# Two products that advance together, chunk by chunk, in a two-block transformer kernel on one Trainium2 core

## The chip, the core and the metric

The kernel runs on one core of one Trainium2 chip. The metric is device time in microseconds (us) of one execution. Engines are named as in the profile: PE is TensorE, DVE is VectorE, ACT is ScalarE, POOL is GpSimd, SP is SyncE.

## What is computed

The input is a sequence of 256 tokens of width 1024 and a context of 256 tokens, all in fp32. The first block has two hybrid layers; the second block has two rounds of feed-forward, mixer, feed-forward.

```
hybrid layer: shift, scale, gate = split(silu(c) @ ada_w + ada_b)
  hx = rms_norm(x) * (1 + scale) + shift          (the same for the context y)
  rq, rk, rv, rg, nq, nk, nv, ng, gq, gk, gv, gg, mg = split(hx @ w_in)
  x += gate * ((g_ret*(ret @ w_ret_o) + g_na*(na @ w_na_o) + g_gqa*(gqa @ w_gqa_o)) @ w_out)
  (the context is updated in layer 0 only)
x = rms_norm(x, final_norm_w)
for i in (0, 1):
  h += 0.5 * swiglu(rms_norm(h), ffn1_w_in[i], ffn1_w_out[i])
  h += mixer_i(rms_norm(h))     i=0: (gelu(y) * rg_lru(conv(r))) @ rec_w_out;  i=1: (u * sg) @ sg_w_out
  h += 0.5 * swiglu(rms_norm(h), ffn2_w_in[i], ffn2_w_out[i])
return rms_norm(h, final_norm)
```

## The kernel before

**Products.** Everything that feeds a product lies transposed: 128 features on the partitions, tokens along the row, eight chunks (KC = 8) of 128 features. A weight tile is 128 x 1024 fp32, that is, one output block of 128 features with its eight chunks. To keep fp32 accuracy, weights and activations are each split into a rounded high part and a low rest, and each chunk is three matmuls into one PSUM bank (`three`, L2211-2217): w_hi by h_hi (L2215), w_hi by h_lo (L2216), w_lo by h_hi (L2217). The moving side has 512 columns (256 tokens and 256 of context) in layer 0 and for keys and values in layer 1, else 256.

**Weight tiles.** SP loads each tile into one of six raw buffers. ACT makes w_hi (L1446) into one of four slots; from the fifth tile on it waits until PE has used the tile four before (semaphore `tile_used`). DVE makes w_lo (L1723), and PE waits for it (`lo_ready`). The schedule puts splits three tiles ahead of the product (`split_ahead`, L329).

**Banks.** Products alternate between the two PSUM banks G[0] and G[1]; a product waits on its first chunk until its bank was evacuated (`g_free`). Sums and spreads of the norms use bank M, the ffn's second up-product the banks S, the adaptive-scale products the banks T.

**Order.** `build_schedule` (L714) records one list of steps, and every engine walks the same list and emits its own part of each step, so the order of the list is the order on each engine. `product` (L368) adds one product: it calls `split_ahead`, then `flush` puts the steps that were held back (evacuations of the product before, squares), then the product in parts of 3, 3 and 2 chunks, between which due and background steps come.

**The start.** Eight `pair` steps bring the adaptive scale and shift of one chunk each: 32 small matmuls of the ada weights (L2289, that is 64 in the trace with their passes), a transpose of the result on DVE (L1751) and an add (L1759, `ada_a`). The first norm's sums are spread over the partitions in M, copied to `rstd` (L1793, in `norm_spread_step`), and `prescale` makes m = x * rstd per chunk (L1741). `normed` then makes h_hi and h_lo of a chunk: h_hi by ACT (L1476 where the chunk's `how` is "dve", L1483 after a full-precision m on ACT), h_lo by DVE (L1867, L1862 before it if `how` is "dve"). Between pairs `keep_busy` lets PE multiply a constant (L2258, n matmuls of 512 columns in fp32r). While `hold` is set, a product comes in parts of 2, 3, 3 chunks, and pair 7 with the `normed` of chunks 6 and 7 (`last_pair`, L758) stands behind the first part of the first product. Until then only tile 0 is split.

**Layers.** `schedule_layer` (L394) makes, for each of four groups of the neighbourhood branch, the products nk, nv (512 columns), nq, ng. The evacuation of nk ("key", to k_s) is ACT L1491 then DVE L1930; that of nv ("value") is ACT L1503 to `stage`. At the end of a layer the eight w_out products are followed by the residual, a square (L1456) and adds of squares; `rms` (L652) then has PE sum the squares over partitions (`norm_mean`, L2327), DVE and POOL take the root (L1801, L1316), and PE spreads it (`norm_spread`, L2345). In layer 1 the eight `normed` steps follow, all chunks with `how` "act". Beside these, POOL loads and adds a bias table (L1277, 128 x 768).

**Feed-forward.** `ffn_step` (PE, L2475) runs 22 rounds of two ups (gate into G, the other into S) and a down. The first two ups are up(0, g) and then up(0, u) (L2528-2529), then the norm's sums and, within up(1, g), its spread. ACT's part splits tile t0+3 after the first up and t0+4 after the second (L1619-1620); DVE's part is at L2090.

**Mixers.** `mixer_out` (L911) makes eight output products from mix_hi and mix_lo (L1663, L2153), whose chunks come out of the scans (recurrent) or the gating (spatial), each followed by a residual add (L1922). In the recurrent mixer, y_act (L1817) evacuates the last y product.

## Time and profile before

| | |
|---|---|
| median of 3 runs | 2062.36 us (2061.68 to 2063.36) |
| the profiled execution | 2060.16 us, span 2058.4 us |
| mean granted PE clock | 0.983 of full speed |
| busy: PE / DVE / ACT / POOL | 1980.5 / 1121.9 / 892.9 / 246.1 us |
| chain that ended last, PE's share | 56%, on 18 + 17 + 17% the three lines of `three` |
| DMA | 289.28 MB, 141 GB/s on average, 317 GB/s in the first fortieth |

The span is that of the trace; the execution's own time is 1.8 us more. Busy time counts compute instructions only; an engine's idle time is what it waited, and the trace names for each idle stretch the instruction whose semaphore ended it. The granted clock is the share of TensorE's full 2.4 GHz that the throttle gave; 0.50 is 1.2 GHz.

### The profile page before, as it was taken

Reading aid. Unit: us, or ns where it says so; the run is one execution under the profiler, and the core shown is the slowest. Engines: PE = TensorE matmul, PEld = TensorE weight load, DVE = VectorE, ACT = ScalarE, POOL = GpSimd, SP = SyncE. Lnnn points to the kernel's source line nnn. Section 1 sums busy time; section 2 is a strip of 40 time slices with the busy share of each in tenths; the row PEclk is TensorE's granted clock in tenths of the full one; section 3 lists DMA queues with packets and bytes.
Section 4 is the critical chain, followed back from the end, with each engine's and each line's share of the span. In section 5 each row is a group of like instructions: output and inputs, shape, how many; then the busy total and the mean of one; then the engine's idle time right before and its main releaser. Section 6 shows DMA issues by size and latency. Waiting matters only on the chain.

```text
span 2058.4 us, 37778 instructions
## 1 busy us (share of the span) xinstructions
PE 1980.5 (96%) x14537; PEld 1782.1 (87%) x14537; DVE 1121.9 (55%) x1798; ACT 892.9 (43%) x1431; POOL 246.1 (12%) x269
## 2 busy tenths in 40 slices
PE   8999999999999899998999999989999999999998
PEld 6777887777787688888899999979999999999998
DVE  6554443445433655446556556875556555675554
ACT  5444231344422544334445445654445444554443
POOL 1000010111012100201121001311001000200000
PEclk9999999999999899999999999989999999999999
DMA  8221433311234323333354555435555555445553
GB/s 317 72 67 63 146 140 133 123 52 62 76 98 144 106 99 103 103 134 103 117 180 145 184 184 173 134 124 180 182 183 190 184 183 184 145 152 175 184 183 113
DMA packets 79432, 289.28 MB, mean 141 GB/s; under 512 B 8912, under 2 KB 9168, under 8 KB 79312
## 3 DMA queue, kind: packets, MB, share of 16 engines
q1 hardware_dynamic: 77616, 281.61, 41.1%
q0 software_dynamic: 1120, 4.72, 0.7%
q8 instruction: 89, 1.46, 0.3%
q10 hardware_dynamic: 576, 1.24, 0.2%
q14 instruction: 31, 0.25, 0.0%
HBM read 286.49 MB, written 1.05 MB: 140 GB/s over the span
## 4 chain that ended last, share of the span: by engine, by line
PE 56%; DVE 5%; ACT 3%; issue 2%; POOL 1%; POOLq 0%; DVEq 0%; ACTq 0%
PE bank L2215 18%; PE bank L2217 17%; PE bank L2216 17%; DVE w_lo L1723 1%; ACT w_hi L1446 1%; PE bank L2404 1%; PE bank L2387 1%; PE bank L2373 1%; ACT h_hi L1462 0%; PE bank L2345 0%; ACT m L1476 0%; PE bank L2444 0%; POOL stats L1316 0%; DVE r_conv L2148 0%; ACT mix_hi L1663 0%
## 5 line engine op out<-in xcount | busy, mean ns | idle before, releaser
L2215 PE MATMUL bank<-h_hi,w_hi 128*128 128x256 f32 (+1 forms) x2720 | 870.5, 320 | 22.4 <-DVE h_lo L1808 7.6
L2217 PE MATMUL bank<-h_hi,w_lo 128*128 128x256 f32 (+1 forms) x2720 | 846.9, 311 | 0.0
L2216 PE MATMUL bank<-h_lo,w_hi 128*128 128x256 f32 (+1 forms) x2720 | 846.4, 311 | 0.0
L1723 DVE TENSOR_TENSOR w_lo<-raw,w_hi 128x1024 fp32r<-128x1024 f32 x484 | 600.4, 1244 | 415.5 <-ACT w_hi L1446 415.0
L1446 ACT ACTIVATE w_hi<-raw 128x1024 fp32r<-128x1024 f32 x484 | 508.9, 1055 | 503.3 <-PE bank L2217 450.0
L2215 PEld LDWEIGHTS bank<-h_hi,w_hi 128*128 128x128 f32 x2720 | 518.8, 191 | 80.4 <-issue 41.7
L2217 PEld LDWEIGHTS bank<-h_hi,w_lo 128*128 128x128 f32 x2720 | 519.3, 191 | 28.9
L2216 PEld LDWEIGHTS bank<-h_lo,w_hi 128*128 128x128 f32 x2720 | 520.2, 191 | 23.3 <-issue 0.4
L2215 PE MATMUL bank<-hid_hi,w_hi 128*128 128x256 f32 x704 | 198.0, 281 | 2.1 <-DVE hid_lo L2071 2.1
L2217 PE MATMUL bank<-hid_hi,w_lo 128*128 128x256 f32 x704 | 197.5, 280 | 0.0
L2216 PE MATMUL bank<-hid_lo,w_hi 128*128 128x256 f32 x704 | 197.2, 280 | 0.0
L1351 POOL TENSOR_TENSOR silu_g<-silu_g,rstd 128x256 f32<-128x256 f32 x88 | 65.3, 742 | 639.9 <-ACT silu_g L1598 639.9
L2215 PEld LDWEIGHTS bank<-hid_hi,w_hi 128*128 128x128 f32 x704 | 132.8, 189 | 3.0 <-DVE w_lo L1723 2.2
L2216 PEld LDWEIGHTS bank<-hid_lo,w_hi 128*128 128x128 f32 x704 | 132.8, 189 | 0.0
L2217 PEld LDWEIGHTS bank<-hid_hi,w_lo 128*128 128x128 f32 x704 | 132.4, 188 | 0.0
L2065 DVE TENSOR_TENSOR hidden<-silu_g,bank 128x256 f32<-128x256 f32 x88 | 37.0, 421 | 122.4 <-POOL silu_g L1351 119.9
L1598 ACT ACTIVATE silu_g<-silu_g 128x256 f32<-128x256 f32 x88 | 36.8, 418 | 154.0 <-DVE silu_g L2056 154.0
L1536 ACT ACTIVATE work<-bank,row_stat 128x512 f32<-128x512 f32 (+1 forms) x96 | 58.3, 612 | 68.9 <-DVE row_stat L1951 68.9
L1546 ACT ACTIVATE work<-bank 128x512 f32<-128x512 f32 (+1 forms) x96 | 45.4, 524 | 79.5 <-PE bank L2387 79.2
L1951 DVE TENSOR_REDUCE row_stat<-bank 128x1 f32<-128x512 f32 (+1 forms) x96 | 53.1, 594 | 34.6 <-PE bank L2373 34.5
L1316 POOL TENSOR_TENSOR stats<-stats,neg_half 128x2 f32<-128x2 f32 (+2 forms) x21 | 24.1, 1146 | 340.4 <-DVE stats L1801 340.4
L1311 POOL TENSOR_TENSOR m<-m,square 128x512 f32<-128x512 f32 (+1 forms) x32 | 33.3, 1042 | 220.3 <-DVE square L1897 220.3
(232 smaller groups left out, 2143.5 us busy)
## 6 DMA issues: line engine op xcount, KB each, us to landing
raw<-in_weights SPq DMA_DIRECT2D x516, 512.0 KB, 3.3
early<-in_first SPq DMA_DIRECT2D x10, 512.0 KB, 13.7
bias<-in_rpb POOLq DMA_DIRECT2D x8, 384.0 KB, 3.4
early_o<-in_first SPq DMA_DIRECT2D x4, 512.0 KB, 16.8
x<-in_tokens SPq DMA_DIRECT2D x2, 512.0 KB, 5.4
x<-in_tokens ACTq DMA_DIRECT2D x2, 512.0 KB, 8.0
work<-in_first SPq DMA_DIRECT2D x2, 512.0 KB, 16.6
out<-cols_out SPq DMA_DIRECT2D x4, 256.0 KB, 2.1
```

The costliest lines, as they stand in the source:

```text
L1311: pool.tensor_tensor(v, v, branch_sum[:, st.dc % 2, 0:st.cols], ALU.add).then_inc(added, 1)
L1351: pool.tensor_tensor(v, v, rstd[:, 0:SEQ], ALU.mult).then_inc(silu_scaled, 1)
L1446: nc.scalar.activation(w_hi[:, n % SPLIT, :], raw[:, t % RAW, :], ACT.Copy).then_inc(hi_ready, 1)
L1536: nc.scalar.activation(probs[:, hp, 0:u.keys], S[use % 2][:, 0:u.keys], ACT.Exp, bias=row_stat[:, 0, i:i + 1], accum_out=row_stat[:, 1, i: ...
L1546: nc.scalar.activation(probs_t[:, hp, 0:u.keys], T[use % 2][:, 0:u.keys], ACT.Copy)\
L1598: nc.scalar.activation(silu_g[:, i % 2, :], silu_g[:, i % 2, :], ACT.Silu).then_inc(silu_ready, 1)
L1723: dve.tensor_tensor(w_lo[:, t % RAW, :], raw[:, t % RAW, :], w_hi[:, SPLIT_NO[t] % SPLIT, :].bitcast(F32), ALU.subtract).then_inc(lo_ready, 1)
L1951: dve.tensor_reduce(row_stat[:, 0, i:i + 1], s[:, 0:u.keys], AX_X, ALU.max, negate=True)\
L2065: dve.tensor_tensor(hidden[:, i % 2, :], silu_g[:, i % 2, :], S[i % 2][:, 0:SEQ], ALU.mult)\
L2215: nc.tensor.matmul(dst, w_hi[:, SPLIT_NO[t] % SPLIT, at], hi, start=start, stop=False, skip_group_check=shared)
L2216: nc.tensor.matmul(dst, w_hi[:, SPLIT_NO[t] % SPLIT, at], lo, start=False, stop=False, skip_group_check=shared)
L2217: return nc.tensor.matmul(dst, w_lo[:, t % RAW, at], hi, start=False, stop=stop, skip_group_check=shared)
```

## The change

1. `product_pair` records two products whose chunks alternate, chunk 0 of the first, chunk 0 of the second, chunk 1 of the first, and so on, in both G banks. It is used for nk and nv of the first group in both layers and for the first two of the eight output products of both mixers. In the four ffns `first_ups` does the same with up(0, g) in G[0] and up(0, u) in S[0].
2. `norm_part` (PE): in both layers, behind the last w_out product, PE multiplies the sum of the earlier squares first and then, in `norm_mean`, only the last square.
3. The adaptive norm's copy of the spread root (L1793) is gone; `prescale` multiplies x by the bank M itself, and the last prescale frees M.
4. In layer 1 chunks 0 and 4 are made by DVE ("dve") rather than by ACT.
5. `keep_busy` takes fp32 operands and counts of 11, 2, 1, 1, 1, 1 where it had 38, 7, 3, 3, 3, 3 in fp32r, and three more such matmuls stand in layer 1 behind the spread.
6. Pair 7 and the `normed` of chunks 6 and 7 stand before the first product; the parts 2, 3, 3 are gone.

```diff
+    def product_pair(self, whats, src, n, norm=None, **fields):
+        jobs = []
+        for i, what in enumerate(whats):
...
+        self.split_ahead(self.tile)
+        self.flush()
+        for k in range(KC):
+            for job in jobs:
+                self.add("product", job=job, at=k, part=1, base=0)
+            if k in (2, 5, 7):
+                self.part_done()
+                self.fill()
+        self.tile += 2
+        return jobs
...
-        key("nk", g)
-        value("nv", g)
+        jobs = s.product_pair(("nk", "nv"), n=BOTH, **src()) if c == 0 else [None, None]
+        key("nk", g, jobs[0])
+        value("nv", g, jobs[1])
...
+        if dc == KC - 1:
+            norm.cols = live
+            norm_part(s, norm)
...
-        st.how = "act" if norm.layer or k % 2 == 0 else "dve"
+        st.how = "dve" if k in ((0, 4) if norm.layer else (1, 3, 5, 7)) else "act"
...
-    def last_pair():
-        normed(s, norm, 6)
-        pair(7)
-        normed(s, norm, 7)
-        s.hold = False
-        s.split_ahead(0)
-
-    s.background = [last_pair]
+    normed(s, norm, 6)
+    pair(7)
+    normed(s, norm, 7)
+    s.hold = False
     for layer in range(DEPTH):
         if layer:
             norm.how, norm.layer = "ada", layer
             s.add("ada_scale", layer=layer)
             rms(s, norm)
+            s.keep_busy(3, s.tile)
...
 def mixer_out(s, what, mixer, weight):
...
+    jobs = s.product_pair((what, what), n=SEQ, src="mix", mixer=mixer)
     for n in range(KC):
-        job = s.product(what, n=SEQ, src="mix", norm=None, mixer=mixer)
+        job = jobs[n] if n < 2 else s.product(what, n=SEQ, src="mix", norm=None, mixer=mixer)
...
-                    dve.wait_ge(m_free, norm.m_spread + 1)
-                dve.tensor_tensor(m[:, k, :], x[:, k, :], rstd[:, :], ALU.mult).then_inc(prescaled, 1)
+                    dve.wait_ge(m_full, norm.m_spread + 1)
+                dve.tensor_tensor(m[:, k, :], x[:, k, :], M[:, :], ALU.mult).then_inc(prescaled if k < KC - 1 else m_free, 1)
...
+                def first_ups():
...
+                    for k in range(KC):
+                        pe.wait_ge(h_lo_ready, norm.chunks[k].h + 1)
+                        for which, bank in (("g", G), ("u", S)):
+                            ins = three(bank[0][:, 0:SEQ], (t0 + ffn_tile(which, 0), k), h_hi[:, k, 0:SEQ], h_lo[:, k, 0:SEQ],
+                                        k == 0, k == KC - 1)
...
-                up(0, "g", first=True)
-                up(0, "u")
+                first_ups()
```

How this moves instructions is shown at three places. **PE at the start, before**: the small L2289 matmuls are the ada pairs (pair 6, then pair 7, whose weights are in `work`), L2215 to L2217 are the chunks of nk; nv begins 26 rows further down.

```order
L2289 MATMUL bank<-early_o,c_silu 32x64 [waits t_free0,first_landed6]
L2289 MATMUL bank<-early_o,c_silu 32x64 x31
L2215 MATMUL bank<-h_hi,w_hi 128x512 [waits h_lo_ready,lo_ready]
L2216 MATMUL bank<-h_lo,w_hi 128x512
L2217 MATMUL bank<-h_hi,w_lo 128x512
L2215 MATMUL bank<-h_hi,w_hi 128x512 [waits h_lo_ready]
L2216 MATMUL bank<-h_lo,w_hi 128x512
L2217 MATMUL bank<-h_hi,w_lo 128x512
L2289 MATMUL bank<-work,c_silu 32x64 [waits t_free1,first_landed7]
L2289 MATMUL bank<-work,c_silu 32x64 x31
L2215 MATMUL bank<-h_hi,w_hi 128x512 [waits h_lo_ready]
L2216 MATMUL bank<-h_lo,w_hi 128x512
```

**PE at the start, after** (the lines of `three` are now L2251 to L2253, those of the pairs L2329):

```order
L2329 MATMUL bank<-early_o,c_silu 32x64 [waits t_free0,first_landed6]
L2329 MATMUL bank<-early_o,c_silu 32x64 x31
L2329 MATMUL bank<-work,c_silu 32x64 [waits t_free1,first_landed7]
L2329 MATMUL bank<-work,c_silu 32x64 x31
L2251 MATMUL bank<-h_hi,w_hi 128x512 [waits h_lo_ready,lo_ready]
L2252 MATMUL bank<-h_lo,w_hi 128x512
L2253 MATMUL bank<-h_hi,w_lo 128x512
L2251 MATMUL bank<-h_hi,w_hi 128x512 [waits lo_ready]
L2252 MATMUL bank<-h_lo,w_hi 128x512
L2253 MATMUL bank<-h_hi,w_lo 128x512
L2251 MATMUL bank<-h_hi,w_hi 128x512 [waits h_lo_ready]
L2252 MATMUL bank<-h_lo,w_hi 128x512
```

Pair 7 stands before the first chunk, and behind the first chunk of nk stands the first chunk of nv with a wait for its own weight tile, ahead of all other chunks.

**ACT at the end of the start, before**: h_hi of chunk 7, the high parts of weight tiles 1 to 5 (raw buffers 1 to 5), and the evacuations of nk (`k_s`) and nv (`stage`).

```order
L1476 ACTIVATE h_hi<-m,ada,ada_a 128x256 [waits a_ready,prescaled]
L1476 ACTIVATE h_hi<-m,ada,ada_a 128x256
L1446 ACTIVATE w_hi<-raw 128x1024 [waits raw_landed1]
L1446 ACTIVATE w_hi<-raw 128x1024 [waits raw_landed2]
L1446 ACTIVATE w_hi<-raw 128x1024 [waits raw_landed3]
L1446 ACTIVATE w_hi<-raw 128x1024 [waits tile_used,raw_landed4]
L1491 ACTIVATE k_s<-bank 128x512 [waits tile_used]
L1446 ACTIVATE w_hi<-raw 128x1024 [waits tile_used,raw_landed5]
L1503 ACTIVATE stage<-bank 128x512 [waits tile_used]
```

After:

```order
L1508 ACTIVATE h_hi<-m,ada,ada_a 128x256 [waits a_ready,m_free]
L1508 ACTIVATE h_hi<-m,ada,ada_a 128x256
L1478 ACTIVATE w_hi<-raw 128x1024 [waits raw_landed1]
L1478 ACTIVATE w_hi<-raw 128x1024 [waits raw_landed2]
L1478 ACTIVATE w_hi<-raw 128x1024 [waits raw_landed3]
L1478 ACTIVATE w_hi<-raw 128x1024 [waits tile_used,raw_landed4]
L1478 ACTIVATE w_hi<-raw 128x1024 [waits tile_used,raw_landed5]
L1523 ACTIVATE k_s<-bank 128x512 [waits tile_used]
L1535 ACTIVATE stage<-bank 128x512 [waits tile_used]
```

The high part of tile 5 (raw buffer 5), which waits until nv's tile has been used, stands now before the evacuation of nk.

**DVE at the same place, before**: the arithmetic of pair 7, h_lo of chunk 7, the low parts, and the last step of nk's evacuation.

```order
L1751 STREAM_TRANSPOSE merge_tanh<-bank 128x64 [waits ada_set,t_full]
L1756 TENSOR_TENSOR ada<-merge_tanh,par 128x2x2 [waits t_free1]
L1759 SCALAR_TENSOR_TENSOR ada_a<-ada,par 128x2 [waits ada_set]
L1862 TENSOR_SCALAR scaled<-m,ada_a,ada 128x256 [waits a_ready,prescaled]
L1862 TENSOR_SCALAR scaled<-m,ada_a,ada 128x256
L1867 TENSOR_TENSOR h_lo<-scaled,h_hi 128x512 [waits h_hi_ready,shift_dve]
L1723 TENSOR_TENSOR w_lo<-raw,w_hi 128x1024 [waits hi_ready] x4
L1930 SCALAR_TENSOR_TENSOR k_s<-bank,k_s 128x512 [waits qk_hi]
L1723 TENSOR_TENSOR w_lo<-raw,w_hi 128x1024 [waits hi_ready]
```

After:

```order
L1783 STREAM_TRANSPOSE merge_tanh<-bank 128x64 [waits ada_set,t_full]
L1788 TENSOR_TENSOR ada<-merge_tanh,par 128x2x2 [waits t_free1]
L1791 SCALAR_TENSOR_TENSOR ada_a<-ada,par 128x2 [waits ada_set]
L1898 TENSOR_SCALAR scaled<-m,ada_a,ada 128x256 [waits a_ready,m_free]
L1898 TENSOR_SCALAR scaled<-m,ada_a,ada 128x256
L1903 TENSOR_TENSOR h_lo<-scaled,h_hi 128x512 [waits h_hi_ready,shift_dve]
L1755 TENSOR_TENSOR w_lo<-raw,w_hi 128x1024 [waits hi_ready] x5
L1966 SCALAR_TENSOR_TENSOR k_s<-bank,k_s 128x512 [waits qk_hi]
L1909 COPY v_s<-bank 128x512 [waits m_full]
L1755 TENSOR_TENSOR w_lo<-raw,w_hi 128x1024 [waits hi_ready]
```

Five low parts (tiles 1 to 5) stand between h_lo of chunk 7 and the evacuation of nk, where four stood. The order of h_lo of chunk 7 and the first of them is the same.

## Rows read from the trace of the kernel before

**Rows 1.** Page, parts 1 (busy) and 5 (groups: busy, mean ns).
```profile
PE 1980.5 (96%) x14537; PEld 1782.1 (87%) x14537; DVE 1121.9 (55%) x1798; ACT 892.9 (43%) x1431; POOL 246.1 (12%) x269
...
L1723 DVE TENSOR_TENSOR w_lo<-raw,w_hi 128x1024 fp32r<-128x1024 f32 x484 | 600.4, 1244 | 415.5 <-ACT w_hi L1446 415.0
```

**Rows 2.** PE's waits, whole span: us in total, times, longest us.
```profile
PE bank L2215 <- DVE h_lo L1867: 6.7, 3, 5.0
```

**Rows 3.** Timeline, PE, the start: start, length, instruction, [idle before <- releaser].
```profile
33.32 0.73 PE L2215 MATMUL bank<-h_hi,w_hi 128*128 128x512 f32 x1
33.85 0.63 PE L2216 MATMUL bank<-h_lo,w_hi 128*128 128x512 f32 x1
34.27 0.63 PE L2217 MATMUL bank<-h_hi,w_lo 128*128 128x512 f32 x1
...
36.11 1.42 PE L2289 MATMUL bank<-work,c_silu 128*32 128x64 f32 x64
...
42.04 0.39 PE L2215 MATMUL bank<-h_hi,w_hi 128*128 128x512 f32 x1
...
47.48 0.47 PE L2215 MATMUL bank<-h_hi,w_hi 128*128 128x512 f32 x1
```

**Rows 4.** Timeline of DVE at the start, same columns.
```profile
37.61 0.25 DVE L1751 STREAM_TRANSPOSE merge_tanh<-bank 128x64 f32<-128x64 f32 x1 [0.93 <-PE bank L2289]
...
40.42 6.31 DVE L1723 TENSOR_TENSOR w_lo<-raw,w_hi 128x1024 fp32r<-128x1024 f32 x4 [0.19 <-ACT w_hi L1446]
46.66 0.68 DVE L1930 SCALAR_TENSOR_TENSOR k_s<-bank,k_s 128x512 fp32r<-128x512 f32 x1
```

**Rows 5.** Timeline of ACT at the start.
```profile
38.35 1.09 ACT L1476 ACTIVATE h_hi<-m,ada,ada_a 128x256 fp32r<-128x256 f32 x2 [2.41 <-DVE ada_a L1759]
39.35 2.94 ACT L1446 ACTIVATE w_hi<-raw 128x1024 fp32r<-128x1024 f32 x3
```

**Rows 6.** Windows of 1 us: busy (count) by engine, PE clock, DMA share, GB/s.
```profile
425.00:426.00 1.00, 0.71 (x6) 0.71 (x7) 0.63 (x2) 0.02 (x1) 0.00 (x0) 0.98 0.00 0
428.00:429.00 1.00, 1.00 (x4) 0.71 (x4) 0.55 (x3) 0.91 (x4) 0.00 (x0) 0.50 0.00 0
429.00:430.00 1.00, 1.00 (x6) 0.55 (x4) 0.68 (x3) 0.11 (x2) 0.00 (x0) 0.81 0.00 0
```

**Rows 7.** Timeline of PE where layer 1 begins.
```profile
679.97 0.76 PE L2215 MATMUL bank<-h_hi,w_hi 128*128 128x512 f32 x1 [5.04 <-DVE h_lo L1867]
...
696.74 0.28 PE L2215 MATMUL bank<-h_hi,w_hi 128*128 128x256 f32 x1
```

**Rows 8.** Timeline of DVE where layer 1 begins.
```profile
674.97 0.69 DVE L1793 COPY rstd<-bank 128x512 f32<-128x512 f32 x1 [3.33 <-PE bank L2345]
675.69 3.52 DVE L1741 TENSOR_TENSOR m<-x,rstd 128x512 f32<-128x512 f32 x3
...
683.14 1.94 DVE L1867 TENSOR_TENSOR h_lo<-m,h_hi 128x512 fp32r<-128x512 f32 x1 [0.32 <-ACT h_hi L1483]
...
689.74 0.69 DVE L1867 TENSOR_TENSOR h_lo<-m,h_hi 128x512 fp32r<-128x512 f32 x1 [0.96 <-ACT h_hi L1483]
```

**Rows 9.** Timeline of PE, spread of the second norm in the first ffn.
```profile
1096.97 0.60 PE L2345 MATMUL bank<-con,stats 128*128 128x128 f32 x4
```

**Rows 10.** Timeline of PE at the recurrent mixer's output products.
```profile
1347.94 0.55 PE L2215 MATMUL bank<-mix_hi,w_hi 128*128 128x256 f32 x1 [3.64 <-DVE y_act L1817]
...
1359.55 0.58 PE L2215 MATMUL bank<-mix_hi,w_hi 128*128 128x256 f32 x1 [0.37 <-DVE mix_lo L2153]
```

**Rows 11.** Timeline of DVE, same place.
```profile
1352.81 0.42 DVE L1817 TENSOR_TENSOR y_act<-bank,rstd 128x256 f32<-128x256 f32 x1
...
1360.02 1.23 DVE L1723 TENSOR_TENSOR w_lo<-raw,w_hi 128x1024 fp32r<-128x1024 f32 x1 [0.52 <-ACT w_hi L1446]
```

**Rows 12.** Timeline of ACT in the second ffn's beginning.
```profile
1385.33 1.06 ACT L1446 ACTIVATE w_hi<-raw 128x1024 fp32r<-128x1024 f32 x1 [0.49 <-PE bank L2217]
```

**Rows 13.** Timeline of PE at the spatial mixer's output products.
```profile
1834.95 0.38 PE L2215 MATMUL bank<-mix_hi,w_hi 128*128 128x256 f32 x1 [1.07 <-DVE mix_lo L2153]
```

More of the change, by code:

```diff
@@ L313, in add, with keep_busy @@
         return step
-    def keep_busy(self, n):
-        self.add("busy", part=n)
+    def keep_busy(self, n, tile=None):
+        self.add("busy", part=n, tile=tile, job=self.uses.get("G", 0))
     def add_after_split(self, kind, **fields):
@@ L655, in rms, with norm_part @@
     norm_spread(s, norm)
+def norm_part(s, norm):
+    norm.m, norm.part = s.use("M"), True
+    s.add("norm_part", norm=norm)
 def norm_mean(s, norm):
+    if norm.m is not None:
+        norm.rows = s.count("rows")
+        s.add("norm_mean", norm=norm)
+        return
     norm.m, norm.rows = s.use("M"), s.count("rows")
@@ L726, in scale @@
             prescale(s, norm, k)
-    s.keep_busy(38)
+    s.keep_busy(11)
     pair(0)
-    s.keep_busy(7)
+    s.keep_busy(2)
     norm_mean(s, norm)
@@ L736, in build_schedule @@
     pair(2)
-    s.keep_busy(3)
+    s.keep_busy(1)
     normed(s, norm, 0)
@@ L742, in build_schedule @@
     pair(3)
-    s.keep_busy(3)
+    s.keep_busy(1)
     normed(s, norm, 2)
@@ L746, in build_schedule @@
     pair(4)
-    s.keep_busy(3)
+    s.keep_busy(1)
     normed(s, norm, 3)
@@ L750, in build_schedule @@
     pair(5)
-    s.keep_busy(3)
+    s.keep_busy(1)
     normed(s, norm, 4)
@@ L2252, in busy_step @@
             def busy_step(st):
-                if st.n == 0:
+                if st.tile is None:
                     pe.wait_ge(set_up_busy, 1)
-                ones = w_hi[:, SPLIT - 1, 0:BOTH]
+                    some = w_hi[:, SPLIT - 1, 0:BOTH].bitcast(F32)
+                else:
+                    pe.wait_ge(lo_ready, SPLIT_NO[st.tile] + 1)
+                    pe.wait_ge(g_free[st.job % 2], st.job // 2)
+                    some = w_hi[:, SPLIT_NO[st.tile] % SPLIT, 0:BOTH].bitcast(F32)
                 for _ in range(st.part):
-                    nc.tensor.matmul(G[0][:, :], ones[:, 0:P], ones, start=True, stop=True)
+                    nc.tensor.matmul(G[st.job % 2][:, :], some[:, 0:P], some, start=True, stop=True)
             def ada_tile_step(st):
@@ L2306, in norm_spread_step, with norm_part_step @@
                 norm_spread(st.norm)
+            def norm_part_step(st):
+                norm = st.norm
+                c = norm.cols
+                pe.wait_ge(m_free, norm.m)
+                pe.wait_ge(sq_added, norm.units[-2].add_n + 1)
+                for b in range(c // P):
+                    nc.tensor.matmul(M[:, b:b + 1], square_of(norm.units[0])[:, P * b:P * b + P], C_("ones"),
+                                     start=b == 0, stop=False, skip_group_check=True)
             def norm_mean(norm):
                 c, halves = norm.cols, norm.units[0].blocks
+                if norm.part:
+                    last_unit = norm.units[-1]
+                    pe.wait_ge(squared, last_unit.n + 1)
+                    for b in range(c // P):
+                        ins = nc.tensor.matmul(M[:, b:b + 1], square_of(last_unit)[:, P * b:P * b + P], C_("ones"),
+                                               start=False, stop=b == c // P - 1, skip_group_check=True)
+                    ins.then_inc(m_full, 1)
+                    return
                 if norm.m:
@@ L2491, in up @@
                     for k in range(KC):
-                        if first:
-                            pe.wait_ge(h_lo_ready, norm.chunks[k].h + 1)
                         if spread and k == 5:
```

40 lines of the change are left out of this document (26 added, 14 removed).

## The prediction

> **What bounds the kernel now.** I read the page's busy times first: PE is busy 1980.5 of 2058.4 us [rows 1], so at most 78 us can be won, and only at places where PE waits. The table of PE's waits comes next; its largest entry among the products is one wait of 5.0 us for h_lo L1867 [rows 2]. Then the timelines around each place that the change touches: the start, the beginning of layer 1, the ffns' first ups, the mixers' outputs. Everywhere else PE runs product after product, so a microsecond lost or won on PE is one of the kernel's. The question at each place is which wait ends last: the activations, the weight tile or the bank.
>
> Two prices recur. A matmul of 512 columns starts every 0.42 us at the lower clock (33.85 to 34.27) and every 0.227 us at the higher (24 of them from 42.04 to 47.48) [rows 3]; a chunk of three is 1.26 or 0.68 us, so each microsecond at half clock costs 0.46. And after an idle of about 2 us near 424 the granted clock was 0.50 (1.2 GHz) in 428 to 429 and 0.81 in 429 to 430 on the way back to full [rows 6], with PE busy all that time. I charge **3.5 us at half clock, 1.6 us of work**, per new long wait, with ends of 0 and of 3.1 (6.8 us at half).
>
> **The start.** Before, nk's first chunk starts at 33.32, pair 7 at 36.11 behind two chunks, and nv runs from 42.04 to 47.48, where nq follows at once [rows 3]. The changed order puts pair 7 ahead of nk, and the second chunk product on PE is nv's chunk 0, which needs w_lo of tile 1. That stands on ACT behind h_hi of chunk 7 and on DVE behind h_lo of chunk 7, as before, so PE stands still until the whole chain of pair 7 is through. The chain: the transpose started at 37.61, 1.50 after pair 7 [rows 4]; h_hi(7) at 38.35, w_hi from 39.35 [rows 5]; w_lo from 40.42 [rows 4]; a w_lo takes 1.24 [rows 1], so tile 1 was whole at 41.7, 5.6 after pair 7's start. Pair 7 now starts at 33.4; but DVE idled only 0.93 before that transpose [rows 4], so the chain moves up by 0.93, to 40.7, unless DVE's queue ahead of it moves too (then at best 33.4 + 5.6 = 39.0). PE does one chunk by 36 and waits some 4.7 us. Then 15 chunk products are left: 10.2 us at the full clock, 51.0; with 1.6 for half clock, 52.6.
>
> Now the banks. Before, nk's bank was evacuated while nv ran. Advanced together, both end at once, and nq needs G[0]. By the order of ACT and DVE, w_hi and w_lo of tile 5 come ahead of k_s. Tile 4's w_hi can start when nk is done, 0.68 before nv, plus about 0.3 until the matmul has drained; two w_hi are 2 x 0.98 (three take 2.94) [rows 5], then w_lo 1.24 [rows 1] and k_s 0.68 [rows 4], with about 0.1 for the handing over: -0.4 + 1.96 + 1.24 + 0.68 + 0.1, or **3.6 us of idle PE** after nv. nq starts at 56.2 against 47.48: +8.8 (52.6 + 3.6 = 56.2, rounded up for the first matmul). After that second wait another 1.6 at half clock: **+10.4**. Ends: 7.1 with no half clock at all, 13.4 with 6.8 us of it twice. ACT's evacuation of nk lies beside w_lo of tile 5 and costs nothing. Smaller keep_busy counts cost and give nothing: those matmuls stood between waits for the ada weights' DMA.
>
> **Beginning of layer 1.** Before, PE starts nk at 679.97 after 5.04 of waiting and nq at 696.74 [rows 7]. norm_part brings nothing: w_lo and the ada tile's arithmetic on DVE held the root anyway. The rstd copy goes, 0.69 [rows 8]. h_lo of chunk 7 stood at 689.74 [rows 8] behind ACT's h_hi (it idled 0.96 for it); with chunks 0 and 4 made on DVE, ACT is relieved and DVE loaded with two more passes, and I leave its end at 690.4. Behind it two chunk products remain, 1.4, and some 0.4 of backlog, 692.2. The bank wait follows as at the start, 3.6: nq at 695.8, 0.9 earlier. Half clock after it, 1.6: **+0.7, taken as +1**. Ends: -2.8 (no loss of clock, and chunk 7 by the 1.5 of the next paragraph earlier), and +5 where the clock stays down until 688 as it did, since 16 chunks at 1.26 don't fit there.
>
> A term inside this: three prescales took 3.52 where an operation of that size took 0.69, so 1.5 too long, and one h_lo took 1.94 instead of 0.69 [rows 8]; both times POOL was adding its bias table. The changed prescale reads M in PSUM and one operand from SBUF. I take no gain from it, since h_lo keeps its two SBUF operands. The Trainium skill, "GPSIMD Engine Reference", section 1, says that GpSimd's SBUF interfaces are shared with VectorE, with contention for DVE instructions that have two SBUF inputs. By that rule the changed prescale would no longer be held up, and layer 1 would come out 1.5 us lower, and the sum at +5.5.
>
> **First ffn.** up(0, g) trickled, with three small waits, and DVE and the root follow; the spread was at 1096.97 [rows 9]. norm_part takes the sums off the path (0.44: half of its matmuls), the pair fills the trickle. The root's step stands behind two w_lo on DVE, 2.5 us [rows 1], so it can't come by more than the DVE chain does. **-1.1**, ends 0 and -2.5.
>
> **Recurrent mixer's output.** The first product waits 3.64 until 1347.94, then for mix_lo up to 1359.55 [rows 10]; it ends with a chunk of 256 columns, 0.64 at half clock (three times half of 0.42), at 1360.2, and the second, eight such chunks less what comes at full clock, near 1365.0. Now the second can't start before G[1] is free, which y_act does at 1352.81 + 0.42 [rows 11]. From 1353.3 fifteen chunks of 256 columns at 0.64 would end at 1362.9, and a part at full clock makes it 1361.7. The third product's bank waits for a residual that stands behind a w_lo at 1360.02 + 1.23 [rows 11], about 1361.7 too. **-3.3**, ends -2.1 and -4.4.
>
> **Other ffns and the spatial mixer.** In the second and fourth ffn up(0, g) had no waits. The pair only makes its tile's slot come free with up(0, u): ACT's w_hi at 1385.33 [rows 12] starts some 2.3 later, then w_lo, the root, the spread: **+0.4 each** (0 to +0.8). The third has two small waits but its DVE chain sets the spread: 0. The spatial mixer loses its wait of 1.07 [rows 13] and keeps 0.25 for a residual: **-0.8** (0 to -1.1).
>
> **Sum.** 10.4 + 1 - 1.1 - 3.3 + 0.8 - 0.8 = +7.0 on the profiled 2060.16, 2067.2. The median of the runs is 2.2 above that execution: **2069.4**. What a measurement here can tell from no change is about 0.2%, 4.1 us, so the edges are 2058.2 and 2066.5.
>
> **Rivals.**
> - *Faster.* Chunk 7's chain decides, at the start. If what stands on DVE ahead of the transpose moves up as well (the copy and the fp32 fillers are gone), tile 1 is whole at 39.0 and PE's wait is 3 us; if then the clock holds, the start costs 7.1 - 1.7 = 5.4, and the pairs elsewhere, at full clock, give their best ends: 5.4 - 2.8 - 2.5 - 4.4 - 1.1 = -5.4, **2057.0**. It takes over once the clock keeps full through waits of 3 us; the row of 428 to 429 [rows 6] speaks against. Chance 0.09.
> - *No difference.* The order is as said, but the clock doesn't fall at the two bank waits: 7.0 - 3.2 = +3.8, **2066.2**; with a start chain at 39.0, less. Chance 0.20.
> - *As forecast.* Chance 0.58.
> - *Worse.* The clock stays at half for 6.8 us after each wait, and layer 1's pair is bound by PE at half clock: 13.4 + 3 - 1.1 - 2.1 + 0.8 - 0.5 = +13.5, **2075.9**. Chance 0.13.
>
> **Range.** 2062 to 2077 leaves out most of the first rival and little above. The forecast's own range is 2066.5 to 2073. Faster 0.09, same 0.20, slower 0.71.
>
> **What would show it.** PE waits of 4 to 5 us for w_lo between nk's and nv's chunk 0 near 36 to 41, and of about 3.6 us for k_s between nv and nq, both at the start and near 692. nq of layer 0 at 56, of layer 1 some 9 us later than before. No gap for mix_lo after 1353 of the old time. The prediction is wrong in its main term if tile 1 is split before pair 7's chain ends, if k_s comes before the high part of tile 5, or if the granted clock is full right after these waits.

## The result and the profile after

| | before | changed |
|---|---|---|
| median of 5 runs | 2062.36 us (2060.56 to 2063.39) | 2074.2 us (2072.25 to 2074.91) |
| ratio | | 1.0056, 95% interval 1.0041 to 1.0071 |
| span of the profiled execution | 2058.4 us | 2073.2 us |
| mean granted PE clock | 0.983 | 0.982 |

The change makes the kernel **11.8 us slower** by the medians. The two profiled executions lie 14.8 us apart, so a ledger of the traces has to come to 14.8.

The page of the changed kernel, its busy times and the group of PE with the new waits (columns as in [rows 1]):

```profile
PE 1989.1 (96%) x14520; PEld 1783.7 (86%) x14520; DVE 1122.0 (54%) x1800; ACT 891.6 (43%) x1429; POOL 244.7 (12%) x269
...
L2251 PE MATMUL bank<-h_hi,w_hi 128*128 128x256 f32 (+1 forms) x2720 | 872.1, 321 | 26.9 <-DVE k_s L1966 7.5
```

PE is busy 8.6 us longer than before (1989.1 against 1980.5) with the same products. Most of it is the fillers, 23.7 us against 16.8, with three new ones in layer 1:

```profile
L2258 PE MATMUL bank<-w_hi 128*128 128x512 f32 x57 | 16.8, 447 | 1.4 <-POOL w_hi L1257 1.4
L2298 PE MATMUL bank<-w_hi 128*128 128x512 f32 x40 | 23.7, 738 | 1.4 <-POOL w_hi L1289 1.4
```

The first line is the kernel before, the second the changed one. The time at half clock, summed over the whole trace, is 69 us before and 76 us after, so the clock makes most of the rest of the 8.6. The remaining 6.2 of the 14.8 is more idle time. PE's waits (us in total, times, longest):

```profile
PE bank L2251 <- DVE k_s L1966: 7.5, 2, 3.9
...
PE bank L2251 <- DVE w_lo L1755: 5.9, 2, 4.0
...
PE bank L2251 <- DVE h_lo L1903: 1.4, 3, 0.6
```

The wait for h_lo in the adaptive norm fell from 6.7 [rows 2] to 1.4, but nothing came sooner by it: the new fillers stand in that time, and nk's first chunk in layer 1 starts 7.14 us after the spread (687.42 to 694.56), before 7.12 (672.85 to 679.97). New are 7.5 for k_s and 4.0 of the 5.9 for w_lo, 11.5 together; a wait of 1.9 for w_lo was there before.

The start, timeline of PE:

```profile
34.02 0.67 PE L2329 MATMUL bank<-early_o,c_silu 128*32 128x64 f32 x28 [2.09 <-issue]
...
34.51 2.00 PE L2329 MATMUL bank<-work,c_silu 128*32 128x64 f32 x63
...
42.07 0.79 PE L2251 MATMUL bank<-h_hi,w_hi 128*128 128x512 f32 x1 [4.04 <-DVE w_lo L1755]
...
59.31 0.77 PE L2251 MATMUL bank<-h_hi,w_hi 128*128 128x512 f32 x1 [3.93 <-DVE k_s L1966]
```

DVE, first pair 6's transpose in the kernel before, then the changed kernel from the same transpose on:

```profile
33.44 0.25 DVE L1751 STREAM_TRANSPOSE merge_tanh<-bank 128x64 f32<-128x64 f32 x1 [1.03 <-PE bank L2289]
```

```profile
34.84 0.25 DVE L1783 STREAM_TRANSPOSE merge_tanh<-bank 128x64 f32<-128x64 f32 x1 [1.71 <-PE bank L2329]
...
37.99 0.24 DVE L1783 STREAM_TRANSPOSE merge_tanh<-bank 128x64 f32<-128x64 f32 x1
...
39.91 0.69 DVE L1903 TENSOR_TENSOR h_lo<-scaled,h_hi 128x512 fp32r<-128x512 f32 x1 [0.45 <-ACT h_hi L1508]
40.79 5.17 DVE L1755 TENSOR_TENSOR w_lo<-raw,w_hi 128x1024 fp32r<-128x1024 f32 x3 [0.18 <-ACT w_hi L1478]
56.20 2.36 DVE L1755 TENSOR_TENSOR w_lo<-raw,w_hi 128x1024 fp32r<-128x1024 f32 x2 [10.24 <-ACT w_hi L1478]
58.48 0.68 DVE L1966 SCALAR_TENSOR_TENSOR k_s<-bank,k_s 128x512 fp32r<-128x512 f32 x1
```

ACT:

```profile
38.72 1.09 ACT L1508 ACTIVATE h_hi<-m,ada,ada_a 128x256 fp32r<-128x256 f32 x2 [1.38 <-DVE ada_a L1791]
39.72 2.94 ACT L1478 ACTIVATE w_hi<-raw 128x1024 fp32r<-128x1024 f32 x3
55.11 2.00 ACT L1478 ACTIVATE w_hi<-raw 128x1024 fp32r<-128x1024 f32 x2 [12.46 <-PE bank L2253]
```

Read them together. Pair 7 starts at 34.51; its transpose at 37.99, without idle before it, behind DVE's own queue, which pair 6 had made 1.4 late (34.84 against 33.44); h_hi of chunk 7 at 38.72; then the high parts at 39.72, the low parts at 40.79; PE's first chunk of nv comes at 42.07 after 4.04 us of waiting for w_lo. At the end of the pair the two high parts (2.00 from 55.11), two low parts (from 56.20) and k_s (58.48) stand one behind the other, and nq starts at 59.31 after 3.93. Before, nq started at 47.48 [rows 3]: 11.8 later. The granted clock (windows, columns as in [rows 6]):

```profile
38.00:41.00 3.00, 0.03 (x1) 0.00 (x0) 2.19 (x8) 2.28 (x4) 0.00 (x0) 1.00 0.37 141
42.00:48.00 6.00, 5.93 (x14) 4.68 (x15) 3.96 (x3) 0.65 (x1) 2.22 (x2) 0.50 0.23 68
60.00:65.00 5.00, 5.00 (x14) 3.84 (x13) 0.00 (x0) 0.00 (x0) 0.00 (x0) 0.50 0.00 0
```

After each of the two waits PE is busy without a gap and yet at 0.50 (1.2 GHz), from 42 to 48 and again from 59 to 65. The clock was already down at the end of each wait, from 41.2 and from 58.3.

Where layer 1 begins, PE:

```profile
687.42 2.08 PE L2403 MATMUL bank<-con,stats 128*128 128x128 f32 x8 [2.45 <-POOL stats L1348]
689.29 4.68 PE L2298 MATMUL bank<-w_hi 128*128 128x512 f32 x6
694.56 0.47 PE L2251 MATMUL bank<-h_hi,w_hi 128*128 128x512 f32 x1 [0.59 <-DVE h_lo L1903]
...
710.73 0.55 PE L2251 MATMUL bank<-h_hi,w_hi 128*128 128x256 f32 x1 [3.61 <-DVE k_s L1966]
```

The spread begins at 687.42, the fillers fill until 694, the pair runs with three short waits for h_lo (0.59, 0.50, 0.30), and then comes the bank wait, 3.61, before nq at 710.73. The recurrent mixer's output products, PE:

```profile
1364.55 0.36 PE L2251 MATMUL bank<-mix_hi,w_hi 128*128 128x256 f32 x1 [3.64 <-DVE y_act L1851]
...
1369.99 0.55 PE L2251 MATMUL bank<-mix_hi,w_hi 128*128 128x256 f32 x1 [4.84 <-DVE y_act L1851]
...
1378.40 0.36 PE L2251 MATMUL bank<-mix_hi,w_hi 128*128 128x256 f32 x1 [0.26 <-DVE x L1958]
```

One wait of 4.84 for y_act, then the pair's fifteen chunks without a gap, and the third product at 1378.40, 13.85 after the first chunk, before 17.17 (1347.94 to 1365.11). PE waited as long in this stretch before, 4.96 in six pieces: what the pair saves is that its chunks run without interruption, and six of them at the full clock (from 1375.87). In the spatial mixer the wait of 1.07 [rows 13] is gone.

How late the changed kernel is against the one before, at the same instruction in both traces, and what each stretch added:

| place | instruction compared | late by | stretch adds | forecast |
|---|---|---|---|---|
| layer 0's first group, past its half clock | k_s of the second group, 73 | 14.6 | +14.6 | +10.4 |
| layer 1's first group | branch gate, 705 | 15.4 | +0.8 | +1 |
| first ffn | silu of round 1, 1098 | 15.7 | +0.3 | -1.1 |
| recurrent mixer up to its output | first output chunk, 1347.94 | 16.6 | +0.9 | not in the sum |
| recurrent mixer's output | sums in the second ffn | 13.55 | -3.05 | -3.3 |
| second ffn | silu of round 1, 1412 | 14.1 | +0.55 | +0.4 |
| third ffn | silu, 1590 | 14.1 | 0 | 0 |
| spatial mixer up to its last gating | last sg matmul, 1830.53 | 15.05 | +0.95 | not in the sum |
| its output and the fourth ffn | end | 14.8 | -0.25 | -0.4 |

### The profile page after: what moved, and what is told of

Same layout as the page of the kernel before. It is cut to its first block, busy times and chain, and to the rows that moved or that the text cites. A ratio compares the mean times of both kernels' runs of the same rounds, so it can differ in the third digit from the quotient of the medians.

```text
span 2073.2 us, 37749 instructions
## 1 busy us (share of the span) xinstructions
PE 1989.1 (96%) x14520; PEld 1783.7 (86%) x14520; DVE 1122.0 (54%) x1800; ACT 891.6 (43%) x1429; POOL 244.7 (12%) x269
## 4 chain that ended last, share of the span: by engine, by line
PE 56%; DVE 5%; ACT 3%; issue 2%; POOL 1%; POOLq 0%; DVEq 0%; ACTq 0%
PE bank L2251 17%; PE bank L2253 17%; PE bank L2252 17%; DVE w_lo L1755 1%; ACT w_hi L1478 1%; PE bank L2462 1%; PE bank L2445 1%; PE bank L2431 1%; PE bank L2403 1%; ACT h_hi L1494 0%; PE bank L2502 0%; POOL stats L1348 0%; DVE r_conv L2184 0%; PE bank L2487 0%; POOL mix_t L1425 0%
## 5 line engine op out<-in xcount | busy, mean ns | idle before, releaser
L2251 PE MATMUL bank<-h_hi,w_hi 128*128 128x256 f32 (+1 forms) x2720 | 872.1, 321 | 26.9 <-DVE k_s L1966 7.5
L2253 PE MATMUL bank<-h_hi,w_lo 128*128 128x256 f32 (+1 forms) x2720 | 848.9, 312 | 0.0
L2251 PEld LDWEIGHTS bank<-h_hi,w_hi 128*128 128x128 f32 x2720 | 521.1, 192 | 84.8 <-issue 37.6
L2253 PEld LDWEIGHTS bank<-h_hi,w_lo 128*128 128x128 f32 x2720 | 521.0, 192 | 29.2
L2252 PEld LDWEIGHTS bank<-h_lo,w_hi 128*128 128x128 f32 x2720 | 521.9, 192 | 23.3
L2251 PE MATMUL bank<-hid_hi,w_hi 128*128 128x256 f32 x704 | 198.1, 281 | 2.1 <-DVE hid_lo L2107 2.1
L2253 PE MATMUL bank<-hid_hi,w_lo 128*128 128x256 f32 x704 | 197.5, 281 | 0.0
L2251 PEld LDWEIGHTS bank<-hid_hi,w_hi 128*128 128x128 f32 x704 | 132.8, 189 | 3.1 <-DVE w_lo L1755 2.2
L2253 PEld LDWEIGHTS bank<-hid_hi,w_lo 128*128 128x128 f32 x704 | 132.4, 188 | 0.0
L1568 ACT ACTIVATE work<-bank,row_stat 128x512 f32<-128x512 f32 (+1 forms) x96 | 58.3, 612 | 68.8 <-DVE row_stat L1987 68.8
```

The costliest lines, as they stand in the source:

```text
L1568: nc.scalar.activation(probs[:, hp, 0:u.keys], S[use % 2][:, 0:u.keys], ACT.Exp, bias=row_stat[:, 0, i:i + 1], accum_out=row_stat[:, 1, i: ...
L2251: nc.tensor.matmul(dst, w_hi[:, SPLIT_NO[t] % SPLIT, at], hi, start=start, stop=False, skip_group_check=shared)
L2252: nc.tensor.matmul(dst, w_hi[:, SPLIT_NO[t] % SPLIT, at], lo, start=False, stop=False, skip_group_check=shared)
L2253: return nc.tensor.matmul(dst, w_lo[:, t % RAW, at], hi, start=False, stop=stop, skip_group_check=shared)
```

## The experiments

Eleven kernels, each timed beside the kernel before on the same chip. Medians in us; the ratio is to the kernel before, with its 95% interval. The changed kernel stands at 2074.2 and 1.0056; it was not timed again beside them. On the three chips used here the kernel before had medians of 2061.94 (the first four), 2062.18 (early to seq0_evac) and 2060.89 (the last three), beside 2062.36, so a difference of medians between chips is good to 1 or 2 us.

| run | edit to the changed kernel | median | ratio |
|---|---|---|---|
| seq0 | nk, nv of layer 0 one after the other | 2060.39 | 0.9992 (0.9983 to 1.0001) |
| seq1 | the same in layer 1 only | 2072.08 | 1.0049 (1.0036 to 1.0062) |
| seqmix | no pair in the mixers | 2076.79 | 1.0075 (1.0062 to 1.0088) |
| sequps | no pair in the ffns | 2071.74 | 1.0047 (1.0034 to 1.0059) |
| early | tile 1 split before pair 7 | 2068.42 | 1.0040 (1.0024 to 1.0055) |
| evac | evacuations before the splits | 2062.68 | 1.0004 (0.9994 to 1.0013) |
| early_evac | both | 2058.46 | 0.9990 (0.9980 to 0.9999) |
| seq0_evac | seq0 and evac | 2054.77 | 0.9965 (0.9952 to 0.9979) |
| seqboth | seq0 and seq1 | 2060.18 | 0.9991 (0.9981 to 1.0002) |
| seq0_oldbusy | seq0 and the fp32r fillers | 2060.21 | 0.9997 (0.9988 to 1.0006) |
| best | seq0, early, evac, paired ups in the first ffn only | 2052.98 | 0.9961 (0.9948 to 0.9975) |

### Undoing one part at a time

**seq0.** One condition more, so that layer 0 makes nk and nv by `product`:

```diff
-        jobs = s.product_pair(("nk", "nv"), n=BOTH, **src()) if c == 0 else [None, None]
+        jobs = s.product_pair(("nk", "nv"), n=BOTH, **src()) if c == 0 and layer else [None, None]
```

> The changed kernel with nk and nv of layer 0 one after the other again; pair 7 still stands ahead of nk, the fillers are still fp32, everything else is as in the changed kernel. Theory A (the pair's waits for nv's tile and for nk's bank, with the half clock behind them, are the whole loss of the start): nk's chunks fill the time of pair 7's chain, nv starts near 42 and nq near 47.5 of the old time, so the start costs 0 to 1 instead of 14.6, and the kernel comes to 2059.5 to 2062.5. Rival B (pair 7's place, the fp32 fillers or the copy that is gone hold the start): nq stays more than 4 us late and the time over 2065.

Measured 2060.39, 13.8 less than the changed kernel. PE in the trace:

```profile
34.40 1.10 PE L2329 MATMUL bank<-work,c_silu 128*32 128x64 f32 x63
...
41.91 0.50 PE L2251 MATMUL bank<-h_hi,w_hi 128*128 128x512 f32 x1 [0.44 <-DVE w_lo L1755]
...
47.68 0.47 PE L2251 MATMUL bank<-h_hi,w_hi 128*128 128x512 f32 x1
```

The wait for tile 1 is still there, ends at the same time (41.91 against 42.07) and costs 0.44, because nk's eight chunks run in it; nq starts at 47.68. Pair 7's new place, the fp32 fillers and the removed copy are all still in this kernel. So the pair of layer 0 is the whole loss of the start: theory A. The parts of the change that touch only layer 1 (its fillers, chunks 0 and 4 on DVE, `norm_part`) were not undone one by one, so what each gives is not shown.

**seq1.** The condition is `c == 0 and not layer`.

> The changed kernel with nk and nv of layer 1 one after the other, the pair of layer 0 kept. Theory A: the bank wait of 3.6 before nq and the half clock behind it (1.4) go, but nv then starts when nk ends and PE is free earlier by what h_lo allows: nk would end near 705 of the new time and nv 5.4 later, so nq starts at about 710.5 as it does now, and only the half clock behind it is won: 0 to 2 us less than the changed kernel, 2072 to 2074. Rival B (the bank wait itself is the price): 3.6 to 5 us less, 2069 to 2070.5.

Measured 2072.08, 2.1 less, with an interval (1.0036 to 1.0062) that overlaps the changed kernel's. In the trace nq comes 22.5 us after the spread (687.14 to 709.67) where the pair needs 23.3 (687.42 to 710.73), and no bank wait or half clock follows. So A holds (0 to 2 less), at its edge; the medians alone would not settle it. The first timeline row is nq's first matmul:

```profile
709.67 0.28 PE L2251 MATMUL bank<-h_hi,w_hi 128*128 128x256 f32 x1
```

**seqmix.** `mixer_out` calls `s.product` for all eight.

> The changed kernel with the mixers' output products one after the other. Theory A (the pairs win 3.1 in the recurrent mixer and 0.75 in the spatial one): 3 to 5 us more than the changed kernel, 2077 to 2079. Rival B (the waits are those of the scan and are only moved from several of mix_lo to one of y_act): no difference, 2073 to 2075.

Measured 2076.79, 2.6 more. The waits for mix_lo are back (2.15, 1.74 and four between 0.23 and 0.36, with 3.65 for y_act ahead). The profiled execution of this run had a span of only 2071.8 us, because at the start, where its instructions are those of the changed kernel, the half clock after each wait was shorter. After the bank wait of 3.93 it was back at full by 63, where the changed kernel's was at half until 65:

```profile
60.00:62.00 2.00, 2.00 (x6) 1.54 (x6) 0.00 (x0) 0.00 (x0) 0.00 (x0) 0.50 0.00 0
63.00:64.00 1.00, 1.00 (x6) 0.74 (x6) 0.00 (x0) 0.00 (x0) 0.00 (x0) 1.00 0.00 0
```

So the two profiles are not to be set against each other for a sum. Within the recurrent mixer's output they can be compared: the third product starts 17.30 us after the first (1360.09 to 1377.39), in the changed kernel 13.85. That and the medians' 2.6 speak for A; the intervals overlap, so the medians alone would not put rival B out.

**sequps.** In `first_ups` the loop over the two products goes outside the loop over the chunks.

> The changed kernel with the ffns' first gate product and first up product one after the other. Theory A (the pair of ups gives nothing in the first ffn, where DVE's adds and low parts set the spread, and costs 0.4 to 0.55 in the second and fourth): 0 to 1.5 us less than the changed kernel, 2072.5 to 2074. Rival B (the pair hides the trickle of h_lo in the first and third ffn): 1 to 2 us more.

Measured 2071.74, 2.5 less, in an interval that overlaps the changed kernel's. In the first ffn the spread comes later without the pair: 1113.35 here against 1112.31, though the first chunk came 0.11 earlier here (1099.36 against 1099.47), so with the pair it is 1.15 sooner. But here PE was at half clock for 13.7 us in this ffn, in the changed kernel for 10.2. The kernel before had no pair either, with 10.2 us at half, and its spread came 13.46 after the first h_lo (1083.51 to 1096.97), the changed kernel's 13.47 (1098.84 to 1112.31). So at equal clock the pair gives nothing in the first ffn, as theory A says: DVE takes the root right behind its two low parts in both. The ledger has a loss of 0.55 in the second ffn. The sum of the four is not settled by these medians.

### The two waits of the start, apart

**early.** The wait for the tile is taken away by splitting it earlier:

```diff
     scale(7)
+    s.add("split", t=SPLIT_TILES[1])
+    s.split_n = 2
     normed(s, norm, 6)
```

> The changed kernel with the split of nv's tile (tile 1) moved ahead of the normed of chunks 6 and 7 and of pair 7, the pairs all kept. Theory A (PE stands still for w_lo of tile 1, which is queued behind pair 7's chain on ACT and DVE): the wait of 4.0 before nv's first chunk goes, and with it the half clock behind it; PE then follows h_lo of chunk 7 (about 40.6) with two chunks left. The pair would end near 48 instead of 55, nq start near 52: 6 to 8 us less than the changed kernel, 2066 to 2068. Rival B (the raw tile has not landed by 33 to 35 because the loads of the ada weights fill the queue): ACT waits for the tile with pair 6's and 7's work behind it, and the time stays over 2071.

Measured 2068.42, 5.8 less: 0.4 above what A gives.

```profile
38.78 0.50 PE L2253 MATMUL bank<-h_hi,w_hi 128*128 128x512 f32 x1 [2.10 <-DVE w_lo L1757]
...
53.21 0.47 PE L2253 MATMUL bank<-h_hi,w_hi 128*128 128x512 f32 x1 [3.93 <-DVE k_s L1968]
```

```profile
46.00:48.00 2.00, 2.00 (x11) 1.65 (x10) 0.00 (x0) 0.00 (x0) 0.95 (x1) 1.00 0.03 12
```

The raw tile had landed. PE still waits 2.10 for w_lo until 38.78, then the pair runs at the full clock, and nq starts at 53.21, 6.1 earlier. The bank wait is unchanged, 3.93. So this wait, with the half clock behind it, was worth about 6.

**evac.** `product` flushes the held-back evacuations before it splits ahead, if a pair of key and value stood before:

```diff
+        if self.paired:
+            self.flush()
         if base == 0:
             self.split_ahead(self.tile)
+        self.paired = False
         self.flush()
```

> The changed kernel with the evacuations of nk and nv put ahead of the splits of the next tiles, in both layers. Theory A (the wait of 3.9 in layer 0 and 3.6 in layer 1 is two splits queued ahead of k_s): each wait falls to 1.4 to 1.7, so 2.2 each; with less half clock up to 2 more: 2068 to 2070. Rival B (the splits that now come later hold the products behind nq): the wait moves to a w_lo two products on, 2072 to 2075.

Measured 2062.68, 11.5 less, over twice what I expected.

```profile
41.85 0.79 PE L2256 MATMUL bank<-h_hi,w_hi 128*128 128x512 f32 x1 [5.50 <-DVE w_lo L1760]
...
54.94 0.47 PE L2256 MATMUL bank<-h_hi,w_hi 128*128 128x512 f32 x1 [0.83 <-DVE k_s L1971]
```

The wait of 5.50 for tile 1 ends where the changed kernel's 4.04 ended. It is longer here, in seq1, seqmix and sequps because pair 7 and nk's first chunk ran at the full clock before it (pair 7 in 1.1 us), in the changed kernel at half (2.00).

```profile
53.47 0.60 ACT L1528 ACTIVATE k_s<-bank 128x512 fp32r<-128x512 f32 x1 [11.04 <-PE bank L2258]
...
54.64 2.00 ACT L1483 ACTIVATE w_hi<-raw 128x1024 fp32r<-128x1024 f32 x2
```

```profile
42.00:45.00 3.00, 3.00 (x8) 2.32 (x8) 3.00 (x2) 0.43 (x1) 2.00 (x2) 0.50 0.21 33
55.00:66.00 11.00, 11.00 (x51) 9.10 (x52) 4.88 (x5) 3.18 (x4) 0.00 (x0) 1.00 0.37 136
```

k_s now goes first on ACT, and the wait for the bank is 0.83 in both layers instead of 3.93 and 3.61, 5.9 less. I had put it at 1.5, because I counted ACT's and DVE's part of the evacuation both after nv; ACT's (0.60 from 53.47) lies in nv's last chunk. The rest is in the main the clock: after 0.83 us of idle it stayed full from 55 to 66, where after 3.93 it was at half from 59 to 65. That cost 2.7 us at the start and 1.4 in layer 1, so 10.0 of the 11.5 are accounted for. The other 1.5 lie within the play of the runs: this kernel's ten executions spread from 2058.75 to 2065.01, and the one in the trace is the fastest. The products behind nq did not wait for their later splits: rival B is out.

**early_evac.**

> Both of the two before. Theory A: the two add up, 2062 to 2065, and what is left of the start's loss (about 2 to 4 us against one product after the other) is the bank wait of 1.5 and the two chunks behind h_lo of chunk 7. Rival B: 2069 or more.

Measured 2058.46, below what A gave. It is 3.7 under the kernel before by the medians on that chip (2062.18) and 2.1 by the ratio (0.10%, interval 0.9980 to 0.9999), so just faster; 15.7 less than the changed kernel, where the two edits alone gave 5.8 and 11.5. nq starts at 49.89, still 2.2 later than with nk and nv one after the other.

### What a better version is made of

**seq0_evac.**

> nk and nv of layer 0 one after the other, the pair of layer 1 kept with the evacuations ahead of the splits. Theory A: 2.2 us less than with the first edit alone, 2058 to 2059.5, and 3 to 4 below the kernel before. Rival B: no less than 2060.

Measured 2054.77, ratio 0.9965: better than A gave. The bank wait fell from 3.62 to 0.82 and the clock is full in all windows from 686 to 702, where seq0 had it at half from 695 to 698.

**seqboth.**

> nk and nv one after the other in both layers, everything else as changed. Theory A (layer 1's pair with the bank wait is a loss of about 2, with the evacuation first a gain of about 3 to 4): 2058 to 2059, 2 less than with the pair kept in layer 1 and 3 to 4 more than with the pair and the evacuations first. Rival B (the order of evacuations and splits helps elsewhere, and the pair of layer 1 itself gives nothing): the same as the version with the evacuations first, 2055.

Measured 2060.18, the same as seq0 (2060.39). From the spread's start nq is reached in 24.07 us (673.90 to 697.97) against 22.38 with the pair (671.73 to 694.11) and 20.49 with the pair and the evacuations first (671.50 to 691.99); the kernel before took 23.89. But seqboth has a stretch of half clock before nq (the last row shown under seqboth), which began between two waits for h_lo of 1.34 and 0.91. In seq1, whose instructions in layer 1 are the same, the clock stayed full at waits of 1.36 and 1.01, and nq came in 22.53. With the pair it took 22.38 in seq0 and 23.31 in the changed kernel. So whether the pair wins anything by itself up to nq is not shown; nor does the expected loss of 2 appear in the medians. With the evacuations first it wins 2.0 to 3.6 up to nq, and 5.4 by the medians, with the half clock behind the bank wait. That is more than A gave, and rival B is out.

```profile
673.90 2.08 PE L2403 MATMUL bank<-con,stats 128*128 128x128 f32 x8 [2.45 <-POOL stats L1348]
...
697.97 0.28 PE L2251 MATMUL bank<-h_hi,w_hi 128*128 128x256 f32 x1
```

And in seq0_evac:

```profile
671.50 2.08 PE L2408 MATMUL bank<-con,stats 128*128 128x128 f32 x8 [2.46 <-POOL stats L1353]
...
691.99 0.35 PE L2256 MATMUL bank<-h_hi,w_hi 128*128 128x256 f32 x1 [0.82 <-DVE k_s L1971]
```

The granted clock in seqboth:

```profile
687.00:692.00 5.00, 4.94 (x12) 3.80 (x13) 4.16 (x8) 3.09 (x5) 0.00 (x0) 0.50 0.01 3
```

**seq0_oldbusy.** The counts 38, 7, 3, 3, 3, 3, without the bitcast.

> nk and nv of layer 0 one after the other, and the fillers of the start again 38, 7, 3, 3, 3, 3 fp32r matmuls. Theory A (the fillers cost and give nothing, since the start is bound by the loads of the ada weights and the chain behind pair 7): the same as without this edit, 2059.5 to 2061.5, with nq at 47.5 to 47.8. Rival B (fp32 fillers keep the clock at full through 33 to 37, where the kernel before was at half): the clock falls there again, nk lags, nq 1 to 2 later.

Measured 2060.21 against 2060.39: no difference. nq starts at 48.0, and the clock is full from 33 to 41 here too, even with PE idle for 1.8 us in between. The form and number of the start's fillers make no difference in this kernel.

**best.**

> Everything that won so far, together: nk and nv of layer 0 one after the other, the pair of layer 1 with the evacuations ahead of the splits, the split of tile 1 ahead of pair 7's chain, the mixers' pairs, and the ups advancing together in the first ffn only. Theory A: the 0.45 wait for tile 1 and 0.4 to 0.55 each in the second and fourth ffn go on top of the last version: 2053 to 2054.5. Rival B (those last steps are within the clock's play): no different from the last version, 2054.5 to 2055.5, or more.

Measured 2052.98 (2052.43 to 2055.32), ratio 0.9961 (0.9948 to 0.9975): 0.39% faster than the kernel before and 21 us faster than the changed one. The interval overlaps that of seq0_evac, so what the last edits add is not shown. The bank wait where layer 1 begins is 0.83 in this version too.

## Why the prediction was right

The sign, the two main waits and their causes were as forecast, and the time, 2074.2, lies in the range of 2062 to 2077. It lies above the narrower range given for the forecast itself, 2066.5 to 2073: +7.0 was too small by 4.8 against the medians and 7.8 against the traces, of which 3 us are that the profiled execution lay 2.2 under the median before and 0.7 above it after. What came at the start is the rival *worse*, at a chance of 0.13, and more than it (14.6 against 13.4); the later stretches fell short of that rival. That the sum still fell inside the range is in part luck.

- **The start, +10.4: right in kind, mis-sized.** PE waited 4.04 for tile 1 and 3.93 for the bank, forecast 4.7 and 3.6. The term is 4.2 short in four pieces. Tile 1 was whole at 42.0, not 40.7, 1.3: the step that failed is that DVE's queue ahead of pair 7's transpose would end when it did before, at 36.68. Pair 6 stalled until 34.02 (before until 32.41), its transpose came 1.4 later, and the queue behind it ended at 37.99. When pair 7 itself ran did not matter: in seq0 it ran from 34.40 at the full clock, and tile 1 was whole at 41.91 all the same. Why pair 6 stalled longer the traces don't name. After the first wait the clock was at half from 42 to 48, not for 3.5 us: the pair's fifteen chunks took 13.3 (42.07 to 55.4) instead of 11.8, 1.5. The bank wait was 0.3 longer. After it PE worked 5.8 us at half clock, which cost 2.7 instead of 1.6, 1.1. That is 4.2.
- **The charge for half clock is the step that failed most, 2.6 of the 4.2.** I took 3.5 us from one stretch, that of [rows 6], as the likely case, and 6.8 as the far end; at the start both waits gave the far end, 6.8 us each, about one of them still within the wait. Runs with the same start differ in it: at the same bank wait seq1 and sequps were at half for 6.8 us too, early and seqmix for 3.4.
- **Layer 1, +1:** measured +0.8, nq 0.6 earlier from the spread and 1.4 of half clock behind it. The bank wait was 3.61, forecast 3.6. Of norm_part nothing is seen, as forecast. Two numbers of the sum's ends don't follow from their own terms: the lower end of layer 1 comes to -2.4 and not -2.8, and *worse* takes +3 for layer 1 where the section gives +5, with which it would be 2077.9, outside the range.
- **First ffn, -1.1: wrong.** The step that failed is that the pair fills the trickle of up(0, g) to any use. The root stands right behind DVE's two low parts (at 1110.66, before at 1095.34), and the spread comes as long after the first h_lo as before, 13.47 and 13.46. The first root came 0.5 less late than the residual before it, by its place norm_part; but the spread of the first norm fell into a half-clock stretch (1.22 us of matmuls, before 0.92), and so did that of the second (0.95 against 0.60). What was left is +0.3.
- **Recurrent mixer, -3.3:** -3.3 up to the third product (13.85 against 17.17), as forecast, and -3.05 up to the second ffn. **Second ffn, +0.4:** +0.55. **Third, 0:** 0.
- **Two stretches that the change doesn't touch gave +0.9 and +0.95**, and were in no term. In the recurrent mixer's beginning the same wait of 1.09 to 1.10 for the root comes in both traces; before, the clock was at half for 3 us after it, in the changed kernel for 6:

```profile
1290.00:1293.00 3.00, 3.00 (x16) 3.00 (x16) 2.45 (x7) 0.00 (x0) 0.00 (x0) 0.51 0.00 0
1293.00:1296.00 3.00, 2.94 (x21) 2.66 (x21) 2.59 (x6) 1.46 (x3) 0.54 (x1) 1.00 0.44 149
```

```profile
1305.00:1311.00 6.00, 5.95 (x24) 5.59 (x24) 4.06 (x10) 0.00 (x0) 0.00 (x0) 0.50 0.08 16
```

Nothing else differs there. In the spatial mixer's beginning, behind the same two waits of 0.80 for h_lo, the clock fell in the changed kernel and not before, and fell again behind the root as it did before. Whether such a stretch is 3 or 6 us long is play that a sum from one trace can't see. The runs of the kernel before spread from 2057.3 to 2065.7 over all that were made; that this play makes that spread is likely by its size, but was not tried.

- **Rivals.** *Faster* would have needed tile 1 at 39.0 and a full clock; neither came. *No difference* needed a full clock after the bank waits; in the run that split evacuations from splits the clock did stay full, but only because the wait itself fell to 0.83.

## What to carry to other kernels

Two products that share their inputs' arrival can only advance together if both weight tiles are there first, and they free their banks together: look at what stands in the evacuating engines' queues behind the pair, and put the evacuations ahead of the next tiles' splits. Where a product alone fills the time of the chain, as nk did at the start, pairing gives nothing and moves a second wait onto TensorE. When costing a new wait of some microseconds on TensorE, add the half clock that follows, 3 us of work at worst here. The bank waits of 0.83 us cost nothing more than themselves; waits between 0.8 and 2.2 us came out both ways.
